# Expert stage of a decoder layer: identity products at ScalarE's table changes, query products in half blocks, two PSUM places for sums and token rows

## The reference

```python
def block(xb):
    q = (xb @ w_q).reshape(TOK_BLK, PEER_HEADS, 2, DK_HALF)
    s = jnp.einsum('thcd,hcnd->thcn', q, sub_keys).astype(jnp.float32)
    s1, i1 = lax.top_k(s[:, :, 0], TOPK)
    s2, i2 = lax.top_k(s[:, :, 1], TOPK)
    cand = (s1[..., :, None] + s2[..., None, :]).reshape(TOK_BLK, PEER_HEADS, TOPK * TOPK)
    cid = (i1[..., :, None] * N_KEYS + i2[..., None, :]).reshape(TOK_BLK, PEER_HEADS, TOPK * TOPK)
    top_s, pos = lax.top_k(cand, TOPK)
    eid = jnp.take_along_axis(cid, pos, axis=-1)
    g = jax.nn.softmax(top_s, axis=-1).astype(xb.dtype)
    hid = jax.nn.gelu(jnp.einsum('thkd,td->thk', u_tab[eid], xb), approximate=False)
    return jnp.einsum('thk,thkd->td', g * hid, v_tab[eid])
```

```python
    xp = xp + peer_ffn(rmsnorm(xp, ffn_norm[l]), ...)
y_prompt = rmsnorm(xp, final_norm)
```

## Time and profile before

| | us |
|---|---|
| median of three runs | 1687.77 |
| lowest and highest of them | 1675.85, 1688.12 |
| span of the profiled execution | 1709.3 |
| PE busy in it | 1404.9 (82%) |
| VectorE busy | 1085.5 (64%) |
| ScalarE busy | 634.5 (37%) |
| POOL busy | 652.7 (38%) |

### The profile page before, as it was taken

One profiled execution on the slowest core, in us unless ns is written; L12 is line 12 of the kernel. 1 busy time (PEld: TensorE's weight loads), 2 busy tenths in 40 slices (PEclk: granted clock), 3 DMA queues, 4 the chain that ended last, 5 costly groups with the idle time before them and its releaser, 6 DMA issues.

```text
span 1709.3 us, 17753 instructions
## 1 busy us (share of the span) xinstructions
PE 1404.9 (82%) x5164; PEld 622.7 (36%) x5164; DVE 1085.5 (64%) x2884; ACT 634.5 (37%) x1889; POOL 652.7 (38%) x703
## 2 busy tenths in 40 slices
PE   8999996768997978888878887777777777777786
PEld 5585663435333434334423232222223222222211
DVE  2459978868000046777766766666668888888654
ACT  2421113445211024344444454444445444444443
POOL 3034333322565653333333333333333333333332
PEclk9999996888998989999999999999999999999999
DMA  9798889999999999999999999999999999999997
GB/s 344 292 357 313 318 318 364 398 411 385 358 362 338 386 375 399 413 409 417 410 423 421 406 416 422 421 421 403 407 422 396 414 422 420 405 419 413 409 406 324
DMA packets 112144, 664.81 MB, mean 389 GB/s; under 512 B 13072, under 2 KB 14336, under 8 KB 52400
## 3 DMA queue, kind: packets, MB, share of 16 engines
q0 software_dynamic: 97824, 571.75, 83.4%
q1 hardware_dynamic: 14224, 91.93, 13.8%
HBM read 658.03 MB, written 5.60 MB: 388 GB/s over the span
## 4 chain that ended last, share of the span: by engine, by line
DMA 37%; PE 37%; issue 8%; ACT 7%; DVE 6%; another core or an unknown queue 3%; POOL 0%; ACTq 0%; SPq 0%; DVEq 0%; POOLq 0%
DMA area_r<-in_uv_tab,eid 36%; PE bank L907 11%; PE bank L627 9%; PE bank L851 4%; PE bank L896 4%; ACT area_c L1003 3%; PE bank L798 2%; DVE area_r L1703 2%; PE bank L558 1%; PE bank L871 1%; ACT L1253 1%; DVE area_x L1711 1%; DMA area_w<-in_w_in 1%; PE bank L767 1%
## 5 line engine op out<-in xcount | busy, mean ns | idle before, releaser
L907 PE MATMUL bank<-area_r,area_c 128*128 128x512 f32 (+1 forms) x1584 | 778.8, 624 | 213.8 <-ACT area_c L1003 212.8
L1873 POOL DMA_INDIRECT area_r<-in_uv_tab,eid x544 | 515.7, 948 | 944.0 <-PE bank L907 590.0
L1703 DVE CUSTOM_DVE_ANT_0 area_r<-area_r,bank 128x1024 f32<-128x1024 f32 x416 | 506.3, 1218 | 288.0 <-DMA area_r<-in_uv_tab,eid 287.3
L907 PEld LDWEIGHTS bank<-area_r,area_c 128*128 128x128 f32 (+1 forms) x1584 | 273.3, 188 | 713.0 <-issue 712.6
L1253 ACT ACTIVATE area_c<-hid 128x1 f32<-128x1 f32 x416 | 84.2, 202 | 538.8 <-DVE hid L1703 538.3
L1694 DVE CUSTOM_DVE_ANT_0 area_r<-area_r,bank 128x1024 f32<-128x1024 f32 x128 | 152.9, 1212 | 25.5 <-DMA area_r<-in_uv_tab,eid 22.7
L627 PE MATMUL bank<-area_w,area_t 128*128 128x384 f32 (+1 forms) x448 | 157.6, 509 | 4.1 <-DMA area_w<-in_w_in 3.5
L1003 ACT ACTIVATE area_c<-ident,area_c 128x128 f32<-128x128 f32 x364 | 146.1, 401 | 34.9 <-ACT area_c L1003 1.1
L1873 POOL DMA_INDIRECT area_r<-in_uv_tab,eidT x128 | 121.4, 948 | 82.0 <-issue 29.3
L1003 ACT ACTIVATE area_x<-bank 128x384 f32<-128x384 f32 (+8 forms) x123 | 49.9, 423 | 212.4 <-remote 59.4
L851 PE MATMUL bank<-area_t,area_w 128*128 128x416 f32 (+1 forms) x448 | 118.8, 418 | 6.1 <-issue 5.2
(11 more groups left out here) (200 smaller groups left out, 1202.6 us busy)
## 6 DMA issues: line engine op xcount, KB each, us to landing
area_w<-in_w_in SPq DMA_DIRECT2D x12, 1536.0 KB, 11.1
area_w<-in_k_cache SPq DMA_DIRECT2D x8, 1920.0 KB
area_w<-in_w_q SPq DMA_DIRECT2D x14, 1024.0 KB, 6.8
area_r<-in_uv_tab,eid POOLq DMA_INDIRECT x544
area_w<-in_w_out SPq DMA_DIRECT2D x4, 2048.0 KB, 11.6
area_w<-in_v_cache SPq DMA_DIRECT2D x4, 1920.0 KB
area_v<-in_v_cache SPq DMA_DIRECT2D x4, 1152.0 KB
area_x<-in_x_p SPq DMA_DIRECT2D x6, 512.0 KB
```

The source lines that it names most:

```text
L907: mm = pe.matmul(acc[0:n, c, :], diag[by_pe(i) % DG][:, 0:n], x_ring[s][:, D + c * 512:D + (c + 1) * 512], start=(i == 0), stop=False, ski ...
L1703: vec.tensor_tensor_reduce(out=u, in0=u, in1=x_cur, scale=1.0, scalar=0.0, op0=ALU.mult, op1=ALU.add, accum_out=hid[t % 2][:, j:j + 1]).th ...
L1873: nc.gpsimd.indirect_dma_start(out=ring[s], out_offset=None, in_=table, in_offset=bass.IndirectOffsetOnAxis(ap=where, axis=0)).then_inc(la ...
```

## The change

It does three things.

1. **Identity products** (`fill_time`, new). Where ScalarE runs an exponential or the root in the stage, PE gets two products of the identity with itself, 512 columns wide, behind the same slot. The result goes to a bank that is not in use and is read by nobody. In tile 1, where a query part stands behind the slot, there are none.
2. **Query halves.** A half of eight products becomes two parts of four; the four parts of a job stand behind slots 1, 3, 6 and 8 of the step, the key scores still behind 13. ScalarE's copies of the queries stay where they were.
3. **Two places** for the sums and the token rows. Tiles 1 and 3 use `bank[0]` and `bank[1]`, tiles 2 and 4 `bank[2]` and `bank[3]`. `read_sum` goes for tiles 1 to 3: the square and the last norm read the sum in PSUM. `start_sum` of the next tile stands behind slot 116 of its predecessor, tile 1's residual behind slot 96, and `set_x` of the next tile behind step 6 (slot 111).

```diff
-        acc = bank[0]
-        x_cur = wide(1, D)
+        SUM_AT, ROWS_AT = {0: 0, 1: 0, 2: 2, 3: 0, 4: 2}, {0: 1, 1: 1, 2: 3, 3: 1, 4: 3}
...
+        KEY_PART = 4
+
         def job_part(j):
-            i, p = HEADS + JOBS_AHEAD + j // TOPK, {3: 0, 8: 1, 13: 2}.get(j % TOPK)
+
+            i, p = HEADS + JOBS_AHEAD + j // TOPK, {1: 0, 3: 1, 6: 2, 8: 3, 13: KEY_PART}.get(j % TOPK)
...
+        def exp_after(t, j):
+
+            return t < SAMP and j % TOPK == 1 and HEADS + 2 <= FIRST[t] + j // TOPK + 1 < HEADS * SAMP
+
+        def root_after(t, j):
+            return j == 5
...
+        REST_AT, NEXT_SUM_AT, NEXT_ROWS_AT = 6 * TOPK, 7 * TOPK + 4, 6
...
+            def fill_time(t, j):
+
+                if t == 1:
+                    pe.wait_ge(s_ready, scores_through(min(HEADS + JOBS_AHEAD + j // TOPK, len(JOBS)) - 1))
+                place = 2 * ROWS_AT[t + 1 if t < SAMP else t - 1] + 1
+                if j // TOPK > NEXT_ROWS_AT:
+                    place = 2 * SUM_AT[t + 1] + 1
...
+                wide_ident = ident[:].unsqueeze(1).to_broadcast([P, 4, P])
+                for _ in range(2):
+                    pe.matmul(half(place).rearrange("p (a b) -> p a b", a=4), ident[:], wide_ident, start=True, stop=True)
...
             def start_sum(t):
                 n = TILES[t][1]
-                if t >= 2:
-                    pe.wait_ge(acc_read, t)
+                if t == 2:
+                    for c in range(2):
+                        pe.wait_ge(q_copied[c], len(JOBS))
+                if t > 2:
+                    pe.wait_ge(y_ready, t - 1)
...
-                        if p < 2:
-                            half_queries(i, p)
+                        if p < KEY_PART:
+                            half_queries(i, p // 2, ks=range(p % 2 * KD // 2, (p % 2 + 1) * KD // 2))
                         else:
                             key_scores(i)
-                if t == 1:
-                    pe.wait_ge(x_added, len(BY_DVE))
-                    start_sum(1).then_inc(rest_added, 1)
+                    elif exp_after(t, j) or root_after(t, j):
+                        fill_time(t, j)
+                    if t == 1 and j == REST_AT:
+                        pe.wait_ge(x_added, len(BY_DVE))
+                        start_sum(1).then_inc(rest_added, 1)
+                    if t < SAMP and j == NEXT_SUM_AT:
+                        start_sum(t + 1)
...
-                if t < SAMP:
-                    read_sum(t)
             load_table(ACT.Sqrt)
...
             def set_x(t):
-                if t >= 1:
+                if t == 1:
                     dve.wait_ge(u_free, UR + SLOTS)
+                if t == 2:
+                    dve.wait_ge(s_ready, len(SCORED))
+                if t > 2:
+                    dve.wait_ge(hid_ready, X_END[t - 2])
                 if t >= 2:
-                    dve.wait_ge(hid_ready, X_END[t - 1])
+                    dve.wait_ge(x_free, by_pe(X_END[t - 2] + NEXT_ROWS_AT * TOPK + 2) + 1)
...
-                if t < SAMP:
-                    set_x(t + 1)
+                    if t < SAMP and h == NEXT_ROWS_AT:
+                        set_x(t + 1)
```

More of the change, by code:

```diff
@@ L838, in queries, with half_queries @@
                     half_queries(i, c, tokens)
-            def half_queries(i, c, tokens=0):
+            def half_queries(i, c, tokens=0, ks=range(KD)):
                 h = JOBS[i][0]
@@ L843, in half_queries @@
                 w = wq_first[h] if i < HEADS else wq_ring[(i - HEADS) % 3]
-                if i < HEADS:
+                if ks[0] == 0 and i < HEADS:
                     pe.wait_ge(wq_in[h], 16)
-                else:
+                elif ks[0] == 0:
                     pe.wait_ge(wq_again[(i - HEADS) % 3], 16 * ((i - HEADS) // 3 + 1))
-                if i >= 1:
+                if ks[0] == 0 and i >= 1:
                     pe.wait_ge(q_copied[c], i)
-                for k in range(KD):
+                for k in ks:
                     mm = pe.matmul(half(4 + c)[:, 0:n], w[:, k, c * P:(c + 1) * P], featT[:, k, a:a + n],
@@ L1357, in _ @@
             exp_head(HEADS + 1)
-            read_sum(0)
+            read_first_sum()
             for g in range(GROUPS):
```

58 lines of the change are left out of this document (32 added, 26 removed).

## The result

The changed kernel took 1690.36 us (median of 22 runs), the kernel before 1687.36 beside it. The ratio is 1.0027 with an interval of [1.0014, 1.0040], and 1.0036 [1.0016, 1.0055] when both were run again later. That is within the 1% which a measurement of this kernel tells from no change, but repeated runs set the sign: some 3 to 5 us slower where I had forecast 7.55 us faster. Its profiled execution has a span of 1687.0 us, and 1688.82 with what lies around it.

What follows compares the result with a forecast made beforehand. The prediction took the expert stage to be bound by its gathers, with only an empty DMA queue costing time. Its terms, -5.8 - 4.5 + 1.25 + 0 + 1.5 = -7.55 us, gave a median of 1680.2, range 1666 to 1694.

Steps and rivals of the forecast that it cites:

- The ceiling: Whole expert stage: 422 GB/s in a clean stretch against 413 overall means 22.5 us lost, the most reordering can win.
- Exponentials, -5.8 forecast: Single-head exponentials in the expert stage: identity products fill PE's idle time and hold the clock, winning 5.8 of 6.3 us.
- The chain from product to clock to PE to POOL: At exponentials: products fill PE's idle 2.00 us, the clock stays full, and POOL's waits fall below 4 us.
- The gauge: POOL's waits in the expert stage: up to 3.50 us free, each us beyond costs 1.5, 1.2 or 0.7 us.
- Changes 1 to 2 and 2 to 3, -4.5 forecast: Tile changes, root included: sum copies and waits leave ScalarE's queue, so 4.5 of 5.0 us lost there goes.
- Change 3 to 4, +1.25 forecast: Behind slot 111 of tile 3: four sample row copies in a row delay slot 112, costing 4.3 us against 3.05 before.
- Quarters, 0 forecast: Query products in quarters behind slots 1, 3, 6 and 8: no net effect, bounds 3 us won and 3 lost.
- Tile 1's start, +1.5 forecast: Start of tile 1, queue dry: slots 2 and 3 come free 2.9 us later behind the first quarter, 1.5 us added.
- rival 2: Clock falls at exponentials as without products, or won time returns as idle time elsewhere: 1686 us, chance 0.20.
- Rival 1: Smoother PE keeps the queue full in tile 1 too, nearly all 22.5 us go: 19 us less, 1669; chance 0.17.
- Rival 3: Identity products run at the lower clock level, a pair takes 3.46 us and delays the next slot: 1705 us, chance 0.08.

Runs made afterwards that it cites:

- the spread copies: The changed kernel with the four sample row copies one by one behind slots 113, 117, 121 and 125 of tile 3: 1687.01 us, ratio 0.9996 to the kernel before.

## Why the prediction was wrong

**The ceiling.** I read 22.5 us of recoverable loss out of 422 against 413 GB/s, taking the cleanest 115 us of the stage as a pace that could be held. The stage as it is cannot hold it. Over slots 128 to 415 some 14.7 us go with instruction loads and output transfers. About 17 of the stage's 35 us lie in tile 1, 14 of them in its first 64 slots, which the change as a whole did not move and whose cause was not looked into. What a better order could win behind tile 1 was 3 us.

**Exponentials, -5.8 forecast.** This is the step that failed. I put the dips of four windows down to the exponentials because they lay beside them. The exponentials cost 1.0 us in all (removed in the kernel before: 4.0 and 3.9 to 2.9), at two of the four places: slots 217 and 233. Of the two windows in tile 3, the one of 75 us had caught two loads of VectorE's instructions (slots 349 and 365), and in the other, 1462.5 to 1485 with 389 GB/s, the dots lose nothing. The chain from product to clock to PE to POOL was right: clock 1.00, pairs of 1.88 us (not over 3), POOL 3.02 us. What failed is its last link, from POOL's wait to lost time: waits of 4.5 to 4.6 us in tile 3 cost nothing that can be told, since the shares that set the landing had work left.

**The gauge.** "1.5, 1.2 and 0.7 us lost for each us beyond 3.5" came from the same windows, and these read too much: in the changed kernel at 1150 to 1170 the formula gives (422 - 383) / 422 x 20 = 1.85 us where the dots slip by 0.86. By the dots, the wait of 9.15 us behind slot 111 went with a loss of 4 us beyond the spread copies.

**Changes 1 to 2 and 2 to 3, -4.5 forecast.** Measured -0.3 each (3.55 to 3.25 and 3.4 to 3.1, means of two traces). This term failed by nearly as much as the first, and for the same reason: its 5.0 us were read off two windows. The copy and the waits did leave ScalarE's queue, but they had cost little. Of the 3.25 us left at the first change two instruction loads and an output transfer are 3.1, and of the 3.1 at the second two loads are 1.9. The forecast of 420 GB/s or more was wrong: 395 and 381.

**Change 3 to 4, +1.25 forecast.** The mechanism was right and the size wrong. I had 4.3 us for the copies against 3.05 before; measured are 6.05 against 3.3, that is +2.75, within the bounds of 0 to 4.8. Dealt out, the same change would have won 1.2 us here (2.0 against 3.3).

**Quarters, 0 forecast** and found. **Tile 1's start, +1.5 forecast:** 14.0 against 13.9 in the first 64 slots, so 0.

**The sum.** By the traces -0.6 for the two tile changes, about 0 for exponentials, +2.75 for the copies and +0.6 in tile 1, +2.8 in all; the medians say +3.0 and +4.8. The traces leave 2 us of the second figure without a place. The time lies inside the range, within the 1% that had 0.73 of the chance, but that is the width of the range and no merit of the sum, whose two large terms, -10.3 together, measured -0.6. Closest comes rival 2, "does not do what it says", at 1686. It was half right: the exponentials' term is 0, but the clock was held. No rival named what happened, a clock that is won and buys nothing. Rival 1 fails on tile 1, which stays at 408 GB/s. Rival 3 is refuted: the pairs ran in 1.88 us, and doubled pairs cost nothing that can be told.

**A page beside the trace.** The Trainium skill's "TensorE: Matmul & The Clock Gate", section "HAM oscillation — how this bites in real kernels", advises, for a matmul loop with few rows whose waits for DMA let the clock fall, to order the work so that TensorE stays warm. Here, in another kind of loop, the clock rose to 1.00 at all of the places shown but one and the kernel was not faster, since TensorE, at 1.95 us of work in a slot of 2.49, was not what the stage waited for.

## What to carry to other kernels

When a stage is bound by transfers, find out what holds a landing back before you shorten a stall of an engine: take the start times of one repeated instruction, subtract the clean pace, and see at which numbers the steps lie and whether they move when the supposed cause is taken out. Windows of bandwidth round a suspected place catch whatever else lies in them, and dip when most shares of a transfer pause though the last one, which sets the landing, is on time. Work that is short in itself can still empty a queue when several pieces stand in a row behind the same wait; one piece per slot cost nothing here.

## What was not expected of the hardware

- A load of 8 KB of VectorE's instructions goes with a slip of 0.95 us in the landing of the gathers, at every 25th slot, or every 16th or 17th when VectorE has more instructions. Twelve or thirteen of them behind tile 1 make 12 us. The slip is that of one of the gather's 16 updates; the other fifteen keep their pace to within 0.02 us in the clearest cases. TensorE's added instructions brought no slip in the run that tried it: their 16 KB loads fell on updates that had time to spare.
- The variants of the changed kernel split into two groups 3 to 6 us apart (1685.6 and 1686.5 without pairs, 1689.8 to 1691.4 with pairs or with 88 waits at the end of TensorE's program that hold nobody). The cause is open, and the kernel before shows no such split.
- The part ahead of the experts varies by 9 us from trace to trace (first dot at 606 to 615 us, and once 634.7; the same kernel 607.2 and 613.7, before 613.5 and 634.7), more than the whole effect of the change.
